# The branch gates' projection in two column halves, low-rank values in four strips, and layer norm's variance in two parts, in a hybrid decoder trunk on one core

## The chip, the cores and the metric

The kernel runs on one core of one Trainium2 chip. The metric is device time of one execution in microseconds (us). The profile is one execution taken by the hardware profiler. Engines are called PE (TensorE, with PEld for its weight loads), DVE (VectorE), ACT (ScalarE), POOL (GpSimd) and SP (SyncE); SP and POOL issue DMAs here. TensorE's clock has two levels, 1.2 and 2.4 GHz; the profile gives the granted clock as a share of the higher one.

## The reference

Two layers (DEPTH = 2) of a decoder trunk, over 256 prompt tokens and 8 sample tokens that share every weight, T = 264 tokens in all, model width D = 2048. Cut to what the change touches:

```python
h = x @ w_in                                   # all mixers and gates at once
gates = sigmoid(gl)                            # gl: 48 columns of h, 3 branches x 16 heads
v = v + (v_first - v) * sigmoid(v0 + (v @ rw_v1) @ rw_v2)   # layer 1 only; rw_v1 is 1024 x 32
merged = sigmoid(g_A) * (o_A @ w_up_a) + sigmoid(g_B) * (o_B @ w_up_b)
x = layer_norm(ALPHA * x + merged @ w_out, g, b)            # over the 2048 channels

def layer_norm(x, g, b):
    mu = x.mean(-1)
    var = square(x - mu).mean(-1)
    return (x - mu) * rsqrt(var + LN_EPS) * g + b
```

## The kernel before

All activations stand transposed: channels on the 128 partitions, the 264 tokens along the free axis. `XT` holds x as KT = 16 tiles of 128 x 264, `H` the projected tiles, everything in float32. A tile of output channels is 16 matmuls (one per tile of the contraction) with 128 x 128 weights and 264 moving columns, accumulated in one of two banks of `PB` (bank 6 or 7 by the tile's parity). A layer has 126 such tiles in a fixed order (`TILES`): `lo`, 8 `v`, 8 `k`, 8 `r`, 8 `z`, 12 `kv`, `gl`, 8 `q`, 8 `zb`, 16 `gb`, 16 `ga`, 16 `up`, 16 `out`. In the trace a float32 matmul has two records.

**The order of the work.** SP streams the weights of one tile after another, in two halves, into two slots of `WT`; a slot is loaded again when the tile that used it is done. PE executes one written list: `project(place)` (L502) issues weight matmuls until a count `UPTO[place]`, which `plan()` works out beforehand; between two such calls stand the small matmuls of the mixers, of the attention and of the norms. So projection matmuls lie as cover between the steps of chains that go from PE to ACT or DVE and back. Each of PE, ACT, DVE and POOL runs its list in order and waits on counting semaphores.

**Branch gates.** Tile `gl` has 48 wanted columns and is computed with 128 x 48 weights. Its 16 matmuls fall in the third of four rounds of the recurrent mixer: two in the step after the second chunk's state, then four groups of three, then two, each group between the small matmuls of L667, L673 and L679 to L686 of one chunk and those of the next. ACT copies the tile to `H`, and after the mixer it takes tanh of it into `SG` (L1050); DVE makes sigmoid of that (L1357). Behind the tanh, ACT stages rows for the attention's compressed blocks (L929, eight copies) and then copies four transposed tiles of values (`VT`), for the first of which PE waits before it transposes the second.

**Low-rank values.** In layer 1, PE multiplies eight `v` tiles by the 128 x 32 tiles of `V1` (L539), all into the same 32 partitions, then sums squares of keys per head (L544, eight matmuls that are already spread over the four strips of 32 columns). ACT copies the 32 rows out; later they are the moving operand of `V2W`, with a contraction of 32 (L579). Behind L544 come DVE's maximum, ACT's square root (L980), DVE's reciprocal (L1222) and PE's L550, with ten projection matmuls as cover.

**Layer norm.** In the `out` stage DVE adds each tile of PSUM to the scaled `XT` (L1603) and keeps a running sum of tiles `LSUM` (L1611). After the last tile come, one behind the other:

```python
mm(PB[:, 0, 0:T], cm(ONES), LSUM[:, :], start=True, stop=False)      # L915
mm(PB[:, 0, 0:T], cm(ONES), XT[:, KT - 1, :], start=False, stop=True)  # L916: sum over channels
# DVE, four instructions of four tiles: XT -= PB[0] / D          (L1616)
# ACT, four instructions of four tiles: LSQ = XT squared         (L1161)
# PE, sixteen matmuls of ONES with the tiles of LSQ into bank 1  (L920)
# DVE: bank 1 / D + LN_EPS (L1618); ACT: sqrt (L1163); DVE: reciprocal (L1620)
# DVE: XT *= 1/std in parts of 1, 3, 4, 4, 4 tiles (L1624)
# ACT: gain and bias, tile by tile                               (L1167)
```

In layer 0, matmul k of the next layer's first tile (`lo`) waits for the gain and bias of tile k. After layer 1, POOL stores y in the same five parts, each when ACT is done with it.

Of the kernel before, what the change touches and what calls it, by code (L numbers as in the profile page):

```python
# [9 lines left out]
ALU = mybir.AluOpType  # L10
# [39 lines left out]
N_DER = 65  # L50
# [46 lines left out]
def plan():  # L97

    upto = {}
    for L in range(DEPTH):  # L100
# [12 lines left out]
        upto[L, "up"] = first + FIRST["out"] * KT  # L113
        upto[L, "out"] = first + N_TILES * KT
# [47 lines left out]
def hybrid_trunk(nc, ins, outs):  # L162
# [4 lines left out]
    with ExitStack() as ctx:  # L167
# [129 lines left out]
        LSQ, LST, LSUM = take(P, KT, T), take(P, T), take(P, T)  # L297

# [14 lines left out]
        def steps(phase, rounds, **engines):  # L313
            for e, names in engines.items():
# [4 lines left out]
        steps("par", 1, v="om half ka")  # L319
# [6 lines left out]
        steps("mix", DEPTH, a="tanh gates pick", t="v0 v1 v2 v3 gates pick", v="gate")  # L326
# [45 lines left out]
        def _(sp):  # L372
# [4 lines left out]
            for n in range(DEPTH * N_TILES):  # L377
# [4 lines left out]
                for half in range(2):  # L382
# [4 lines left out]
                    if n == 0 and half == 1:  # L387
                        load_x(3)

        @block.gpsimd  # L390
        def _(po):
# [83 lines left out]
            for i, j in parts:  # L475
                on(po, "ln_a", DEPTH - 1, f"aff{j - 1}")
                dma(y_t[:, i:j, :], XT[:, i:j, :], st_y)
            po.wait_ge(st_y, 80)
# [7 lines left out]
        def _(pe):  # L486
# [44 lines left out]
            for L in range(DEPTH):  # L531
# [1210 lines left out]
```

## Time and profile before

| | us |
|---|---|
| median of 3 runs (lowest to highest) | 2359.83 (2357.12 to 2361.86) |
| the profiled execution, its own time | 2359.26 |
| its span, first to last instruction | 2357.6 |
| PE busy | 2292.0 (97%) |
| weight loads (PEld) busy | 1853.9 |
| DVE busy | 635.9 (27%) |
| ACT busy | 358.2 (15%) |
| POOL busy | 131.8 (6%) |
| mean granted clock of TensorE | 0.990 |

Busy time is the union of an engine's records. The chain that ended last is followed back from the last instruction to what released each step; its shares tell which engine the end of the program hangs on. The stretches with PE idle are few and short, and the ends of the two layers are the longest of them.

### The profile page before, as it was taken

How to read it: one execution, taken by the hardware profiler on the slowest of the kernel's cores; microseconds unless marked ns; L12 is line 12 of the kernel's file. 1: busy time of each engine (PE TensorE's matmuls, PEld its weight loads, DVE VectorE, ACT ScalarE, POOL GpSimd, SP SyncE). 2: the span in 40 equal slices, each digit the busy share in tenths (PEclk: the TensorE clock that was granted, in tenths of full speed). 3: DMA queues.
4: the chain of work that ended last, by engine and by line, in shares of the span. 5: the costliest groups of instructions: out<-in, count | busy, mean ns of one | idle time of the engine just before them, and what ended most of it. 6: DMA issues, size and time to landing. Idle time of an engine off the chain costs nothing.

```text
span 2357.6 us, 39271 instructions
## 1 busy us (share of the span) xinstructions
PE 2292.0 (97%) x17604; PEld 1853.9 (79%) x17604; DVE 635.9 (27%) x1156; ACT 358.2 (15%) x939; POOL 131.8 (6%) x233
## 2 busy tenths in 40 slices
PE   8999999999999999999899999999999999999995
PEld 7887878778786788888788778777788767888884
DVE  0133322227316310111201424223363253001112
ACT  0111111120104311000201211111211052100002
POOL 0000000011011210000000000000101103000000
PEclk9999999999999999999999999999999999999997
DMA  6533333346333454444344332333554325444441
GB/s 217 182 124 99 121 126 109 127 147 241 131 119 103 149 174 145 153 144 147 102 148 143 107 110 97 122 107 112 202 205 144 106 91 173 149 152 152 143 143 73
DMA packets 86792, 326.41 MB, mean 138 GB/s; under 512 B 11808, under 2 KB 11824, under 8 KB 84448
## 3 DMA queue, kind: packets, MB, share of 16 engines
q1 hardware_dynamic: 73152, 266.44, 33.9%
q0 software_dynamic: 13472, 57.46, 6.9%
q8 instruction: 139, 2.28, 0.4%
q14 instruction: 29, 0.24, 0.0%
HBM read 313.42 MB, written 18.82 MB: 141 GB/s over the span
## 4 chain that ended last, share of the span: by engine, by line
PE 95%; DVE 2%; ACT 2%; DMA 1%; issue 0%; POOL 0%; DVEq 0%; ACTq 0%; SPq 0%; POOLq 0%
PE PB L521 76%; PE PB L762 3%; PE PB L593 1%; PE PB L491 1%; PE PB L636 1%; PE PB L650 1%; PE PB L809 1%; PE PB L920 1%; PE PB L854 1%; ACT ARENA L929 1%; DMA WT<-in_w_all 1%; PE PB L673 1%; PE PB L679 1%; PE PB L667 0%; PE PB L806 0%
## 5 line engine op out<-in xcount | busy, mean ns | idle before, releaser
L521 PE MATMUL PB<-XT,WT 128*128 128x264 f32 (+1 forms) x6016 | 1422.6, 392 | 13.5 <-DMA WT<-in_w_all 7.0
L521 PEld LDWEIGHTS PB<-XT,WT 128*128 128x128 f32 (+1 forms) x6016 | 1119.9, 190 | 237.1 <-issue 36.1
L521 PE MATMUL PB<-H,WT 128*128 128x264 f32 x2048 | 456.5, 386 | 3.1 <-DVE H L1595 3.1
L521 PEld LDWEIGHTS PB<-H,WT 128*128 128x128 f32 x2048 | 389.0, 190 | 70.3 <-issue 3.8
L929 ACT ACTIVATE ARENA<-PB 128x512 f32<-128x512 f32 (+5 forms) x197 | 88.6, 475 | 357.0 <-PE PB L625 115.1
L1592 DVE SCALAR_TENSOR_TENSOR H<-H,PB 128x264 f32<-128x264 f32 x32 | 13.7, 430 | 305.2 <-PE PB L521 305.2
L1195 DVE COPY SHO<-PB 128x9 f32<-128x9 f32 x66 | 11.0, 167 | 266.2 <-ACT H L951 214.7
L393 POOL DMA_DIRECT2D out<-in_c_win x16 | 8.2, 512 | 1279.0 <-DVE ARENA L1350 1279.0
L1161 ACT ACTIVATE ARENA<-XT 128x1056 f32<-128x1056 f32 x8 | 8.7, 1084 | 458.4 <-DVE XT L1616 458.0
L951 ACT ACTIVATE H<-PB,PD 128x264 f32<-128x264 f32 x58 | 27.9, 480 | 287.9 <-PE PB L521 287.9
L1603 DVE SCALAR_TENSOR_TENSOR XT<-PB,XT 128x264 f32<-128x264 f32 x32 | 13.9, 433 | 207.1 <-PE PB L521 207.1
L966 ACT ACTIVATE H<-PB 128x264 f32<-128x264 f32 x64 | 25.0, 391 | 293.7 <-PE PB L521 293.5
L762 PE MATMUL PB<-ARENA 128*128 128x288 f32 x256 | 62.9, 407 | 2.2 <-ACT ARENA L929 2.2
L762 PEld LDWEIGHTS PB<-ARENA 128*128 128x128 f32 x256 | 48.5, 190 | 16.2 <-ACT ARENA L929 3.0
L1112 ACT ACTIVATE ARENA<-ARENA 128x128 f32<-128x128 f32 (+1 forms) x128 | 56.4, 445 | 23.1 <-DVE ARENA L1510 23.1
L393 POOL DMA_DIRECT2D ARENA<-in_c_sel x64 | 40.1, 627 | 294.5 <-issue 294.5
L1331 DVE TENSOR_TENSOR ARENA<-ARENA,PB 128x1024 f32<-128x1024 f32 x32 | 39.1, 1222 | 58.7 <-PE PB L653 58.7
L957 ACT ACTIVATE H<-PB 128x264 f32<-128x264 f32 x56 | 21.8, 390 | 214.2 <-PE PB L521 214.2
L1350 DVE SCALAR_TENSOR_TENSOR ARENA<-PB,ARENA 128x64 f32<-128x64 f32 x64 | 15.2, 279 | 144.0 <-PE PB L679 143.8
L1322 DVE TENSOR_TENSOR ARENA<-ARENA,CM 128x512 f32<-128x512 f32 x32 | 22.2, 692 | 88.2 <-PE PB L625 63.3
L636 PEld LDWEIGHTS PB<-ARENA 64*64 64x64 f32 x1024 | 32.6, 134 | 11.0 <-issue 11.0
L650 PEld LDWEIGHTS PB<-ARENA 64*64 64x64 f32 x1024 | 32.3, 134 | 11.0 <-issue 8.3
(277 smaller groups left out, 1685.9 us busy)
## 6 DMA issues: line engine op xcount, KB each, us to landing
WT<-in_w_all SPq DMA_DIRECT2D x504, 512.0 KB, 4.7
out<-in_c_win POOLq DMA_DIRECT2D x16, 512.0 KB, 5.4
ARENA<-in_c_cmp POOLq DMA_DIRECT2D x64, 128.0 KB, 4.2
ARENA<-in_c_sel POOLq DMA_DIRECT2D x64, 128.0 KB, 3.3
ARENA<-in_c_win POOLq DMA_DIRECT2D x32, 256.0 KB, 3.7
ARENA<-in_states POOLq DMA_DIRECT2D x4, 1024.0 KB, 9.2
out<-ARENA POOLq DMA_DIRECT2D x4, 1024.0 KB, 4.5
ARENA<-in_w1d POOLq DMA_DIRECT2D x4, 1024.0 KB, 5.1
```

What stands on the lines that cost most here:

```text
L393: po.dma_start(out, in_).then_inc(s, 16)
L491: return tr(out, in_, ident[0:in_.shape[0], 0:in_.shape[0]])
L521: ins = mm(PB[0:m, bank, 0:T], WT[:, s, k, 0:m], x, start=start, stop=stop)
L593: ins = mm(PB[ra, 2 + 2 * w + i, c * P:c * P + P], src[ra, w, c * C:c * C + C], AR[ra, w * NCH + c].rearrange("p x n -> p (x n)"), start=T ...
L636: ins = mm(PB[ra, 0, q * C:q * C + C], LM[oa, q, :], XX[oa, q, :], start=True, stop=True)
L650: mm(PB[other(ra), 4, cols], XX[ra, 2 * NCH + q, :], YY[ra, q, :], start=True, stop=True)
L762: ins = mm(PB[:, 3 * (s // 8) + gp, 0:CMP_N], W1D[:, s, :], x, start=s % 8 == 0, stop=s % 8 == 7)
L929: return act(out, in_, ACT.Copy)
L951: act(a_tile(L, kind, t), psum, ACT.Copy, scale=PD[:, L, OM + t:OM + t + 1]).then_inc(scaled, 1)
L966: act(H[:, t if kind == "ga" else GB_AT[t], :], psum, ACT.Tanh, scale=0.5).then_inc(tile_out[s], 1)
L1112: ins = act(x, x, ACT.Exp, bias=NM[u % 3][:, t, i:i + 1], accum_out=RSM[u % 3][:, t, i:i + 1])
L1331: v(f"z{j}", tt(XX[:, :, :], XX[:, :, :], z, ALU.add))
```

## The change

Four things are done.

- **Branch gates.** Tile `gl` is computed with 64 weight columns (48 wanted, 16 zeros), even k into output rows 0 to 63, odd k into rows 64 to 127. ACT copies all 128 rows out. Before the tanh, ACT copies the lower 48 rows of the second half into `SG` and DVE adds the first half to it.
- **Low-rank values.** The eight matmuls of L539 go to four strips of 32 output rows, so that `VV1` has 128 rows with four partial sums, and `V2W` is stored four times below itself: the contraction of L579 has 128 rows.
- **Layer norm.** After `out` tile 12, PE sums the first 12 tiles (HEAD = 12) over the channels ("head"). DVE subtracts the mean of these 1536 channels from them into `LSQ`, ACT squares that, and after eight matmuls of tile 14 PE adds the twelve up in four strips of 32 columns, three each ("hvar"). ACT scales this by 1/32 into `LVA`, and after four matmuls of tile 15 PE sums it with ONES over all partitions, which starts bank 1 ("fold"). After the last tile: the sum as before; DVE centres tiles 12 to 15 first, in two instructions; ACT squares them in two; DVE makes the shift of the mean and its square times 1536 ("d", "e"); PE adds four matmuls of squares and one of the shift with the identity to bank 1; DVE meanwhile centres tiles 0 to 11 in three instructions. ACT's square root reads PSUM with LN_EPS as its bias and 1/D as its scale, and L1618 is gone. Gain and bias of tiles 12 to 15 move from ACT to DVE, behind the last of L1624.
- **Stores.** y goes out from SP's queue instead of POOL's, in parts of 3, 3, 3, 3 and 4 tiles.

```diff
@@ plan
+        out = first + FIRST["out"] * KT
+        upto[L, "head"], upto[L, "hvar"], upto[L, "fold"] = out + (HEAD + 1) * KT, out + (HEAD + 2) * KT + 8, out + (HEAD + 3) * KT + 4
@@ sync
+            for i, j in stores:
+                if j <= SPLIT:
+                    on(sp, "ln_a", DEPTH - 1, f"aff{j - 1}")
+                else:
+                    on(sp, "ln_v", DEPTH - 1, "affv")
+                sp.dma_start(y_t[:, i:j, :], XT[:, i:j, :]).then_inc(st_y, 16)
@@ tensor, project
+                    if kind == "gl":
+                        rows, start, stop = slice(k % 2 * C, k % 2 * C + C), k < 2, k >= KT - 2
+                    ins = mm(PB[rows, bank, 0:T], WT[:, s, k, 0:rows.stop - rows.start], x, start=start, stop=stop)
@@ tensor
-                        ins = mm(PB[0:32, 1, 0:T], V1[:, k, :], H[:, V0 + k, :], start=k == 0, stop=k == 7)
+                        ins = mm(PB[32 * (k % 4):32 * (k % 4) + 32, 1, 0:T], V1[:, k, :], H[:, V0 + k, :], start=k < 4, stop=k >= 4)
...
+                project(L, "head")
+                on(pe, "ln_v", L, f"sum{HEAD - 1}")
+                mark("ln_t", L, mm(PB[:, 2, 0:T], cm(ONES), LSUM[:, :], start=True, stop=True), "head")
+                project(L, "hvar")
+                for k in range(HEAD):
+                    on(pe, "ln_a", L, f"hq{k // 4}")
+                    rows = slice(32 * (k % 4), 32 * (k % 4) + 32)
+                    ins = mm(PB[rows, 3, 0:T], cm(ONES)[:, 0:32], LSQ[:, k, :], start=k < 4, stop=k >= HEAD - 4)
+                mark("ln_t", L, ins, "hvar")
+                project(L, "fold")
+                on(pe, "ln_a", L, "hv")
+                mm(PB[:, 1, 0:T], cm(ONES), LVA[:, :], start=True, stop=False)
...
-                for k in range(KT):
-                    if k % 4 == 0:
-                        on(pe, "ln_a", L, f"sq{k // 4}")
-                    ins = mm(PB[:, 1, 0:T], cm(ONES), LSQ[:, k, :], start=k == 0, stop=k == KT - 1)
-                mark("ln_t", L, ins, "var")
+                for k in range(HEAD, KT):
+                    on(pe, "ln_a", L, f"sq{(k - HEAD) // 2}")
+                    mm(PB[:, 1, 0:T], cm(ONES), LSQ[:, k, :], start=False, stop=False)
+                on(pe, "ln_v", L, "e")
+                mark("ln_t", L, mm(PB[:, 1, 0:T], ident, LDQ[:, :], start=False, stop=True), "var")
@@ scalar
-                mark("mix_a", L, act(SG[:, :], H[0:48, GL, :], ACT.Tanh, scale=0.5), "tanh")
+                mark("mix_a", L, copy(SG[:, :], H[C:C + 48, GL, :]), "half")
+                on(sc, "mix_v", L, "gl")
+                mark("mix_a", L, act(SG[:, :], SG[:, :], ACT.Tanh, scale=0.5), "tanh")
...
+                mark("ln_a", L, act(LST[:, :], PB[:, 1, 0:T], ACT.Sqrt, bias=PD[:, L, EPS:EPS + 1], scale=1.0 / D), "sqrt")
@@ vector
+                own("mix_a", "half")
+                mark("mix_v", L, tt(SG[:, :], SG[:, :], H[0:48, GL, :], ALU.add), "gl")
...
+                for q in range(2):
+                    centred(HEAD + 2 * q, 2, f"ycb{q}")
+                mark("ln_v", L, stt(LDA[:, :], PB[:, 0, 0:T], -1.0 / D, LMA[:, :], ALU.mult, ALU.add), "d")
+                own("ln_v", "d")
+                mark("ln_v", L, stt(LDQ[:, :], LDA[:, :], HEAD * P, LDA[:, :], ALU.mult, ALU.mult), "e")
+                for q in range(3):
+                    centred(4 * q, 4, f"yca{q}")
...
+                own("ln_v", "yn4")
+                for t in range(SPLIT, KT):
+                    ins = ts(XT[:, t, :], XT[:, t, :], PT[:, L, LNG + t:LNG + t + 1], PT[:, L, LNB + t:LNB + t + 1], ALU.mult, ALU.add)
+                mark("ln_v", L, ins, "affv")
```

## Rows read from the trace of the kernel before

**Rows 1.** The page: the chain that ended last, shares of the span by engine

```profile
PE 95%; DVE 2%; ACT 2%; DMA 1%; issue 0%; POOL 0%; DVEq 0%; ACTq 0%; SPq 0%; POOLq 0%
```

**Rows 2.** Chain of waits, end of layer 0: start us, us, what

```profile
1139.90 9.80 PE PB L521 x44
...
1150.08 0.43 DVE ARENA L1611
...
1150.64 0.68 PE PB L915 x2
...
1154.24 7.40 PE PB L920 x32
...
1162.59 1.81 DVE ARENA L1620
...
1165.65 10.51 PE PB L521 x38
```

**Rows 3.** Timeline, end of layer 0: start us, us, engine, line, operation, count, idle before

```profile
1151.81 4.75 DVE L1616 SCALAR_TENSOR_TENSOR XT<-PB,XT 128x1056 f32<-128x1056 f32 x4 [1.31 <-PE PB L916]
...
1157.70 1.28 ACT L1163 ACT_TABLE_LOAD   x1
...
1164.42 4.83 DVE L1624 TENSOR_TENSOR XT<-XT,ARENA 128x264 f32<-128x264 f32 x5
...
1174.92 0.48 ACT L951 ACTIVATE H<-PB,PD 128x264 f32<-128x264 f32 x1 [1.54 <-PE PB L521]
```

**Rows 4.** Timeline, end of layer 1

```profile
2319.84 0.43 DVE L1603 SCALAR_TENSOR_TENSOR XT<-PB,XT 128x264 f32<-128x264 f32 x1 [6.35 <-PE PB L521]
...
2324.36 10.12 PE L920 MATMUL PB<-ARENA,CM 128*128 128x264 f32 x32 [2.46 <-ACT ARENA L1161]
...
2335.43 1.80 DVE L1620 RECIPROCAL ARENA<-ARENA 128x264 f32<-128x264 f32 x1 [0.49 <-ACT ARENA L1163]
...
2338.64 7.59 ACT L1167 ACTIVATE XT<-XT,PT 128x264 f32<-128x264 f32 x15 [0.29 <-DVE XT L1624]
...
2346.63 0.53 POOL L393 DMA_DIRECT2D out<-XT  x1 [1.46 <-ACT XT L1167]
```

**Rows 5.** Windows: us; busy of PE, PEld, DVE, ACT, POOL; granted clock; DMA share; GB/s

```profile
1165.00:1170.00 5.00, 4.35 (x12) 3.13 (x13) 4.26 (x4) 4.71 (x10) 0.00 (x0) 0.66 0.00 0
...
2324.00:2326.00 2.00, 1.64 (x4) 1.33 (x5) 2.00 (x3) 1.84 (x3) 0.00 (x0) 0.50 0.00 0
2348.00:2349.00 1.00, 0.00 (x0) 0.00 (x0) 0.00 (x0) 0.00 (x0) 0.00 (x0) 0.50 1.00 418
```

**Rows 6.** Groups by line and form: busy us, mean ns

```profile
L1397 DVE SCALAR_TENSOR_TENSOR H<-PB,H 128x528 f32<-128x528 f32 x2 | 1.4, 708 | 2.5 <-PE PB L728 2.5
...
L1080 ACT ACTIVATE ARENA<-H 128x528 f32<-128x528 f32 x2 | 1.3, 644 | 0.9 <-DVE H L1397 0.9
```

**Rows 7.** Windows from a group's first start to the next group's (L736, L854)

```profile
598.29:599.32 1.03, 1.03 (x17) 0.41 (x17) 0.00 (x0) 1.03 (x1) 0.00 (x0) 1.00 0.00 0
734.61:735.09 0.48, 0.48 (x5) 0.34 (x6) 0.41 (x1) 0.48 (x3) 0.00 (x0) 1.00 0.00 0
```

**Rows 8.** Window: a `gl` group (L521's PE, PEld, clock, DMA); timeline: an uncovered L673

```profile
420.17:421.64 1.47, 1.47 (x6) 0.66 (x6) 1.00 0.94 228
...
512.64 0.45 PE L673 MATMUL PB<-ARENA 64*64 64x64 f32 x8 [0.38 <-ACT ARENA L929]
```

**Rows 9.** Layer 1: window over L539 and L544, then timeline, ACT and DVE

```profile
1295.80:1300.36 4.56, 4.56 (x33) 2.20 (x32) 0.96 (x4) 3.77 (x7) 0.00 (x0) 1.00 0.67 225
...
1296.80 1.28 ACT L974 ACT_TABLE_LOAD   x1
...
1301.73 1.80 DVE L1222 RECIPROCAL ARENA<-ARENA 128x264 f32<-128x264 f32 x1 [0.78 <-ACT ARENA L980]
```

**Rows 10.** Timeline behind the mixer of layer 0, ACT and PE

```profile
518.32 3.41 ACT L929 ACTIVATE ARENA<-H 64x128 f32<-64x128 f32 x8 [0.62 <-PE PB L491]
...
522.43 0.52 PE L491 MATMUL PB<-CM,H 128*128 128x128 f32 x3 [1.59 <-ACT VT L929]
```

More of the change, by code:

```diff
@@ L49 @@
 OM, W0H, A0H, V0H, KA1 = 0, 33, 41, 49, 57
-N_DER = 65
+N_DER = 66
+EPS = 65
+HEAD = 12
+SPLIT = 12
 IDENT, ONES, BLOCK = 0, 1, 2
@@ L297, in hybrid_trunk @@
         LSQ, LST, LSUM = take(P, KT, T), take(P, T), take(P, T)
+        LMA, LDA, LDQ, LVA = (take(P, T) for _ in range(4))
         d_const, d_par, d_toep, d_lora, d_w1, d_page = (sem(n) for n in (
@@ L325, in hybrid_trunk @@
                             + " ".join(f"lm{j + 1} z{j}" for j in range(1, LEVELS)) + f" z{LEVELS} st " + " ".join(f"d{c} s{c}" for c in ch)))
-        steps("mix", DEPTH, a="tanh gates pick", t="v0 v1 v2 v3 gates pick", v="gate")
+        steps("mix", DEPTH, a="half tanh gates pick", t="v0 v1 v2 v3 gates pick", v="gl gate")
         steps("mixv", DEPTH, a="v0 v1 v2 v3")
@@ L338, in hybrid_trunk @@
         steps("xa", DEPTH, a="scale")
-        steps("ln", DEPTH, t="mu var", v=" ".join(f"sum{i}" for i in range(1, KT - 1)) + " " + " ".join(f"yc{q}" for q in range(4)) + " eps rs "
-              + " ".join(f"yn{q}" for q in range(5)), a=" ".join(f"sq{q}" for q in range(4)) + " sqrt " + " ".join(f"aff{i}" for i in range(KT)))
+        steps("ln", DEPTH, t="head hvar mu var", v=" ".join(f"sum{i}" for i in range(1, HEAD)) + " hm" + "".join(f" hc{q}" for q in range(3)) + " "
+              + " ".join(f"sum{i}" for i in range(HEAD, KT - 1)) + " ycb0 ycb1 d e" + "".join(f" yca{q}" for q in range(3)) + " rs "
+              + " ".join(f"yn{q}" for q in range(5)) + " affv", a="hq0 hq1 hq2 hv sq0 sq1 sqrt " + " ".join(f"aff{i}" for i in range(SPLIT)))
         parts = [(0, 1), (1, 4), (4, 8), (8, 12), (12, 16)]
+        stores = [(0, 3), (3, 6), (6, 9), (9, 12), (12, 16)]
         def on(eng, key, it, name):
@@ L473, in _ @@
                         dma(SVS[odd][:, m, 2:4, :], c_win[L, b, :, 2:4, :], d_att[odd])
[L475 to L478, printed above, removed]
+            po.wait_ge(st_y, 16 * len(stores))
             po.wait_ge(st_shift, DEPTH * 16)
@@ L510, in project @@
                     if kind == "lo" and L:
-                        on(pe, "ln_a", L - 1, f"aff{k}")
-                    m, bank, start, stop = P, 6 + s, k == 0, k == KT - 1
+                        if k < SPLIT:
+                            on(pe, "ln_a", L - 1, f"aff{k}")
+                        else:
+                            on(pe, "ln_v", L - 1, "affv")
+                    rows, bank, start, stop = slice(0, P), 6 + s, k == 0, k == KT - 1
                     if kind == "up":
@@ L1667, in packed @@
     out["lora"] = c(np.concatenate([i["rw_w2"], i["rw_a2"]], 1))
-    out["v2w"] = c(i["rw_v2"][0])
+    out["v2w"] = c(np.tile(i["rw_v2"][0], (4, 1)))
     out["v1"] = c(i["rw_v1"][0].reshape(8, P, 32).transpose(1, 0, 2))
```

52 lines of the change are left out of this document (33 added, 19 removed).

## The prediction

> **What bounds the kernel now.** I read the page's chain first: 95% of the span hangs on PE [rows 1]. A microsecond is gained only where PE issues less, or where it stands idle waiting for a chain of other engines. Next the chain of waits at the end of layer 0, which shows the price of a projection matmul, 9.80/22 = 0.445 us (two records each), and the longest stretch without projection work: the last `out` matmul ends at 1149.70, L915 starts at 1150.64, and `lo` starts at 1165.65, 15.95 us later [rows 2]. In it PE works 1.15 + 7.40 us and otherwise waits. The timeline gives the steps beside the chain [rows 3], the end of layer 1 the same chain ahead of the stores [rows 4], the windows the granted clock [rows 5]. Then I looked for what the trace shows of matmuls side by side in strips of the array [rows 7], and at the places of the two small edits [rows 8 to 10].
>
> The sum is made against the profiled execution's own 2359.26 us (its span is 2357.6). That is 0.57 below the median of the runs shown. Their spread is 4.7 us, and 0.2%, about what a measurement of this kernel can tell from no change, is 4.7 us too.
>
> **Branch gates.** A group of three narrow matmuls takes 1.47 us, as three full ones would (3 x 0.445 and the joints), so 48 columns save nothing now [rows 8]. Do halves run side by side? Two matmuls of 128 x 64 weights and 256 columns took 0.48 us from start to the next group, where one alone needs 256/264 x 0.445 = 0.43; eight in four strips with 264 columns took 1.03, two rounds of 0.445 and 0.14 for the joints [rows 7]. So I count rounds. The sixteen matmuls fall in groups of 2, 3, 3, 3, 3, 2; alternating halves make each one round shorter: 6 x 0.445 = 2.67. For joints I take off 0.17 and use 2.5 a layer, **-5.0** in all (ends: -5.3, and 0 if halves don't overlap). The groups are cover for copies on ACT. Where nothing covers such a copy, PE stands idle 0.38 ahead of L673 [rows 8]; a group of about 1.0 still covers that.
>
> The trace shows the joint of a switch to strips and back at about 0.07 each. The Trainium skill ("TensorEngine Tiling (Array Packing)", Key Properties) says that changing the tiling mode, unlike changing the tile, drains TensorE. The trace agrees that a joint costs something. If a drain costs more at the new joints than at those of rows 7, the time is the second rival's, 2352.0; by the sum it is 2347.0.
>
> The price of this edit is one ACT copy, one DVE addition and two hand-overs ahead of the tanh: 0.43 (a neighbour's 3.41/8 [rows 10]), 0.43 (L1611 [rows 2]) and 0.04, so 0.9 us. ACT stands idle for 0.62 behind the tanh, until PE has transposed the state's vectors, so 0.28 shows. Behind it are queued eight copies, 3.41, then the copy of the first value tile for which PE already waits 1.59 [rows 10]. **+0.6** for two layers (0 to 1.8, if the cover of 0.62 were gone). DVE's copies behind its own part come up to 0.9 later, and what follows them waits for states by DMA. POOL's and SP's queues are not touched here.
>
> **Low-rank values (layer 1).** L539 and L544 together take 4.56 us; as two groups of eight in strips they take 2 x 1.03: -2.5 [rows 7, 9]. What is late next: L544 needs the last square, ready at 1296.8, early enough. But ACT's queue (table load from 1296.80, tanh, two copies, table load, square root) no longer fits. With 1.28 for a load and some 0.42 for each of the others the root ends near 1301.05, the reciprocal (1.80) near 1302.9, while PE, ten matmuls behind 1297.9, stands there at 1302.6: +0.3. Net **-2.2** (-2.5 to -1.5; 0 without overlap). The eight matmuls of L579 go from 32 to 128 rows with the same columns: 0, and for the range 0.19 each way for each, the weight load that such a joint may show or hide.
>
> **Layer norm, inside the `out` stage.** New on PE, per layer. "Head" stands at a tile's boundary and needs DVE's addition and running sum of the tile just finished; that is the wait ahead of L915, 1150.64 - 1149.70 = 0.94 idle, and 0.445 for the matmul [rows 2]. "Hvar" is twelve in four strips, 1.03 + 0.445 = 1.48 [rows 7]; its squares are ready in time, since DVE (0.43 and 3 x 1.2) and ACT need some 6 us and 24 matmuls (10.7) lie between. "Fold" is 0.445. With joints 3.4, **+6.8** for two layers. The ends are 3.3 and, if strips ran one after another, 12 x 0.445 + 1.9 = 7.2 a layer. Weights are no issue: SP's loads hang on finished tiles as before.
>
> **The end of layer 0.** Count from the last `out` matmul, t = 0. The sum is done at 2.1 as before. DVE then has two centrings of 528 columns, 0.708 each [rows 6], "d" and "e", 0.43 each, and three centrings of 1056; four of those take 4.75, so a step is 1.17 [rows 3]. With issue overlaps: 2.1 + 0.65 + 0.65 + 0.46 + 0.36 + 3.6 = 7.8. Meanwhile ACT squares at 2.9 and 3.5, 0.64 each [rows 6]; PE starts at 3.6, five matmuls with the closing latency of L920 (7.40 - 7.12) end at 6.1; ACT's table load (1.28 [rows 3]) is done at 5.5; the root ends at 6.5. DVE is later: the reciprocal starts at **7.8**, and DVE takes PE's place as what the end hangs on. Before it was 1162.59 - 1149.70 = 12.9 [rows 2]. The rest, to `lo`'s first matmul, is 3.06 in both. **-5.05**.
>
> The granted clock: `lo` runs from 1165.65 to 1174.90, 9.25 instead of 7.12. The clock is at 1.2 GHz from shortly after its start (0.66 over 1165 to 1170, so 3.4 us low, 1.7 lost [rows 5]); the rest is the wait for the second tile's gain. PE had stood idle 4.0 us before it. After the change it stands idle 10.9 - 6.1 = 4.8, and the clock may be down already when `lo` starts. I take +0.5. The ends are -1.7 (no low stretch) and +1.0 (a loss like that of L920 in layer 1, 10.12 - 7.40 = 2.7 [rows 2, 4]).
>
> **The end of layer 1.** Before, the clock fell in the gap ahead of L920, and sixteen matmuls took 10.12 instead of 7.40 [rows 2, 4, 5]; the reciprocal started at 2335.43 - 2319.80 = 15.6. After: 7.8 at the high clock; at the low one five matmuls cost 2.2 more, 1.0 of which shows beyond DVE, 8.8. The first gap is shorter now (1.5 us instead of 2.5), so I take 8.1: **-7.5**. Behind the reciprocal's start ACT takes up its second tile at 3.2 and ends tile 11 at 3.2 + 11 x 0.51 = 8.9; DVE ends its last scaling at 1.84 + 4.83 = 6.7 [rows 3, 4] and tiles 12 to 15, at 0.43 each at most, by 8.4. Before, ACT ended at 10.8 [rows 4]. The last data moved until 2349.0, 13.6 after the reciprocal's start [rows 4, 5]. Now two stores of together 0.95 MB leave almost at once at 8.9. At 418 GB/s [rows 5] that is 2.3, with a start like SP's weight loads, 1.0 to 2.0 behind the issue: 12.3 to 13.3. **-0.6** (-1.3 to +0.5).
>
> By the Trainium skill ("DMA: Bandwidth & Descriptors", SWDGE vs HWDGE) first bytes come in about 0.6 us from SP against about 1 us from POOL, an estimate of 0.4 us less. No run here yet shows a store from SP.
>
> **The sum:** -5.0 + 0.6 - 2.2 + 6.8 - 5.05 + 0.5 - 7.5 - 0.6 = -12.45, so 2359.26 - 12.45 = 2346.8; with a part of the distance to the median, **2347.0**.
>
> **Rivals.**
> - *The clock eats part of it* (10%). Both ends run their five matmuls at 1.2 GHz and `lo` has the long low stretch: +1.0, +0.7 and +0.5, so 2349.2. For it: the drop in rows 5 in a gap of 2.5. Against it: layer 0 had the same gap and stayed high.
> - *Joints cost more than I take* (8%). If each of the six `gl` groups and every other new joint loses about 0.25, a matmul's tail, that is 12 groups of `gl` and some 8 other places, 20 x 0.25 = 5.0: 2352.0. Against: 0.14 for a whole group [rows 7].
> - *Less at the ends than the sum has* (8%): the clock stays up in `lo`, stores overlap better and strips lose nothing: -2.2, -0.7, -0.5, so 2343.6.
> - *Slower* (3%): matmuls of new strips don't run side by side because they accumulate in one bank. It decides at the first group of `gl`: -5.0 and -2.2 fall away, "hvar" costs 3.8 more twice: 2347.0 + 7.2 + 7.7 = 2361.9, slower than before by 2.6, and 2364.1 with the clock's 2.2. Both groups of rows 7 speak against it, and both accumulate in strips of one bank.
> - *The change doesn't do what it says* (2%): the ends stay, because the root still comes last behind something (a second table load, 1.28): then some 2 us less gain, 2349.
>
> **How the numbers follow.** The forecast has 69%. The bounds of its terms, not all at once, give 2342 to 2352; the rivals of the same sign lie inside or near. Range 2341.5 to 2353, about 8 in 10 with the spread of a median. Faster by over 0.2% needs less than 2355: 0.90, within 0.2% 0.07, slower 0.03.
>
> **What would show it.** Steps: `gl`'s groups at 1.0 us; L539's successor and L544 in 2.1 with a wait of some 0.3 before L550; PE idle 0.9 before "head" in each layer; DVE without a gap from the sum to the reciprocal, which starts 7.8 behind the last `out` matmul. Wrong: ACT's root ending later than DVE's last centring, a first `gl` group still at 1.47, `lo` above 11 us, or the last store landing more than 14 behind the reciprocal.

## The result, and the profile of the changed kernel

The changed kernel takes **2346.82 us** (median of five runs), the one before 2360.61 (five runs, 2357.12 to 2362.08): a ratio of 0.9942 with a 95% interval of 0.993 to 0.9953, so 13.8 us faster by the medians. Four of the five runs of the changed kernel lie between 2345.11 and 2347.16 (their own median is 2346.78); the fifth took 4759.01 us, was slow for a reason that nothing on record shows, and is not in the ratio. The profiled execution took 2347.16 us (span 2345.5), where the one of before took 2359.26 (span 2357.6): 12.1 us less in both, against a sum of 12.45.

The page's chain answers to [rows 1]. PE holds 94% of it. POOL and its queue, in the chain before, are gone from it, since the stores now go through SP's queue:

```profile
PE 94%; DVE 2%; ACT 2%; DMA 1%; issue 0%; ACTq 0%; SPq 0%; DVEq 0%
```

In the new file L521 is L540, L539 and L544 are L559 and L564, L550 is L570, L915/L916/L920 are L948/L949/L952, L1611/L1616/L1620/L1624 are L1659/L1671/L1682/L1686, L1163/L1167 are L1205/L1210, L929 is L962, L491 is L505.

The end of layer 0, timeline (start us, us, engine, line, operation, count, idle before); it answers to [rows 2, 3]:

```profile
1153.16 0.68 PE L948 MATMUL PB<-ARENA,CM 128*128 128x264 f32 x2 [0.96 <-DVE ARENA L1659]
...
1154.33 1.32 DVE L1671 SCALAR_TENSOR_TENSOR XT<-PB,XT 128x528 f32<-128x528 f32 x2 [1.31 <-PE PB L949]
1155.07 1.26 ACT L1203 ACTIVATE ARENA<-XT 128x528 f32<-128x528 f32 x2 [13.73 <-DVE XT L1671]
...
1155.77 3.51 PE L952 MATMUL PB<-ARENA,CM 128*128 128x264 f32 x8 [1.48 <-ACT ARENA L1203]
...
1159.75 0.48 ACT L1205 ACTIVATE ARENA<-PB,PD 128x264 f32<-128x264 f32 x1 [2.13 <-PE PB L954]
1160.27 1.80 DVE L1682 RECIPROCAL ARENA<-ARENA 128x264 f32<-128x264 f32 x1 [0.31 <-ACT ARENA L1205]
...
1163.32 13.05 PE L540 MATMUL PB<-XT,WT 128*128 128x264 f32 x45 [3.61 <-ACT XT L1210]
```

And the end of layer 1, which answers to [rows 4]:

```profile
2319.54 1.32 DVE L1671 SCALAR_TENSOR_TENSOR XT<-PB,XT 128x528 f32<-128x528 f32 x2 [1.31 <-PE PB L949]
...
2320.78 0.42 DVE L1676 SCALAR_TENSOR_TENSOR ARENA<-PB,ARENA 128x264 f32<-128x264 f32 x1
...
2320.98 2.05 PE L952 MATMUL PB<-ARENA,CM 128*128 128x264 f32 x8 [1.48 <-ACT ARENA L1203]
2321.23 0.43 DVE L1678 SCALAR_TENSOR_TENSOR ARENA<-ARENA 128x264 f32<-128x264 f32 x1
...
2321.58 3.58 DVE L1671 SCALAR_TENSOR_TENSOR XT<-PB,XT 128x1056 f32<-128x1056 f32 x3
...
2323.51 0.48 ACT L1205 ACTIVATE ARENA<-PB,PD 128x264 f32<-128x264 f32 x1 [0.67 <-PE PB L954]
2325.08 1.79 DVE L1682 RECIPROCAL ARENA<-ARENA 128x264 f32<-128x264 f32 x1
...
2328.27 5.59 ACT L1210 ACTIVATE XT<-XT,PT 128x264 f32<-128x264 f32 x11 [0.29 <-DVE XT L1686]
2329.40 5.29 SPq L404 DMA_DIRECT2D out<-XT  x5
```

The same code runs twice, and the two places differ in one row: the eight records of L952 take 3.51 in layer 0 and 2.05 in layer 1. In layer 1 no DVE row carries an idle time from L1671's first to the reciprocal at 2325.08, and the root ended at 2323.99, 1.1 earlier: DVE sets the end. In layer 0 the root came last, and the reciprocal waited for it (0.31 idle, ACT named).

The windows (columns as in [rows 5]) show why the eight records differ; 1155 to 1160 against 2320 to 2324, then the start of the next layer, then the stores:

```profile
1155.00:1160.00 5.00, 3.95 (x10) 2.85 (x10) 4.92 (x7) 2.79 (x4) 0.00 (x0) 0.66 0.33 134
...
1165.00:1170.00 5.00, 5.00 (x15) 3.92 (x15) 3.33 (x6) 4.06 (x9) 0.00 (x0) 0.60 0.00 0
...
2320.00:2324.00 4.00, 2.49 (x10) 1.82 (x10) 3.97 (x7) 3.02 (x4) 0.00 (x0) 1.00 0.00 0
2336.00:2337.00 1.00, 0.00 (x0) 0.00 (x0) 0.00 (x0) 0.00 (x0) 0.00 (x0) 0.50 1.01 410
```

Where the 12.1 us come from, by stretches between the same events in both profiled executions (us):

| stretch | before | after | difference |
|---|---|---|---|
| layer 0: start to the last mixer matmul | 517.06 | 514.70 | -2.36 |
| to the first gate selection (tanh chain) | 13.41 | 14.03 | +0.62 |
| to the `out` stage | 504.37 | 504.92 | +0.55 |
| `out` stage | 114.85 | 118.55 | +3.70 |
| last `out` matmul to the reciprocal | 12.90 | 8.07 | -4.83 |
| first gain to the end of `lo`'s first tile | 9.99 | 10.97 | +0.98 |
| layer 1: low-rank values | 9.21 | 7.20 | -2.01 |
| mixer | 381.69 | 378.75 | -2.94 |
| tanh chain, and what follows up to `out` | 518.26 | 518.44 | +0.18 |
| `out` stage | 114.84 | 118.57 | +3.73 |
| last `out` matmul to the reciprocal | 15.63 | 7.67 | -7.96 |
| reciprocal to the end of the span | 22.17 | 20.42 | -1.75 |

The two stretches left out (2.30 ahead of the first gain, 120.9 ahead of the values) are the same within 0.02.

### The profile page after: what moved, and what is told of

It is laid out like the page before. It is cut to its first block, busy times and chain, and to the rows that moved or that the text cites. A ratio compares the mean times of both kernels' runs of the same rounds, so it can differ in the third digit from the quotient of the medians.

```text
span 2345.5 us, 39317 instructions
## 1 busy us (share of the span) xinstructions
PE 2282.0 (97%) x17616; PEld 1847.0 (79%) x17616; DVE 648.1 (28%) x1179; ACT 355.9 (15%) x937; POOL 128.7 (5%) x228
## 4 chain that ended last, share of the span: by engine, by line
PE 94%; DVE 2%; ACT 2%; DMA 1%; issue 0%; ACTq 0%; SPq 0%; DVEq 0%
PE PB L540 76%; PE PB L782 3%; PE PB L505 1%; PE PB L613 1%; PE PB L670 1%; PE PB L656 1%; PE PB L829 1%; PE PB L874 1%; ACT ARENA L962 1%; DMA WT<-in_w_all 1%; PE PB L693 1%; PE PB L699 1%; PE PB L687 0%; PE PB L826 0%; PE PB L596 0%
## 5 line engine op out<-in xcount | busy, mean ns | idle before, releaser
L540 PE MATMUL PB<-XT,WT 128*128 128x264 f32 (+1 forms) x6016 | 1418.6, 392 | 13.7 <-DMA WT<-in_w_all 6.9
L540 PEld LDWEIGHTS PB<-XT,WT 128*128 128x128 f32 (+1 forms) x6016 | 1119.2, 190 | 233.9 <-issue 34.8
L540 PE MATMUL PB<-H,WT 128*128 128x264 f32 x2048 | 457.7, 386 | 3.1 <-DVE H L1641 3.1
L540 PEld LDWEIGHTS PB<-H,WT 128*128 128x128 f32 x2048 | 388.8, 190 | 71.0 <-issue 4.7
L962 ACT ACTIVATE ARENA<-PB 128x512 f32<-128x512 f32 (+5 forms) x197 | 88.5, 475 | 353.2 <-PE PB L645 115.2
L1638 DVE SCALAR_TENSOR_TENSOR H<-H,PB 128x264 f32<-128x264 f32 x32 | 13.7, 429 | 305.2 <-PE PB L540 305.2
L1649 DVE SCALAR_TENSOR_TENSOR XT<-PB,XT 128x264 f32<-128x264 f32 x32 | 13.8, 433 | 204.8 <-PE PB L540 204.8
L1197 ACT ACTIVATE ARENA<-ARENA 128x1056 f32<-128x1056 f32 x6 | 6.5, 1084 | 415.5 <-DVE ARENA L1665 415.2
```

The source lines that it names most:

```text
L540: ins = mm(PB[rows, bank, 0:T], WT[:, s, k, 0:rows.stop - rows.start], x, start=start, stop=stop)
L962: return act(out, in_, ACT.Copy)
```

## The experiments

Those of one group share their runs of the kernel before; each is set against the change (2346.82, ratio 0.9942) and read by its stretches too. The medians of the kernel before lie between 2359.78 and 2362.13 in the groups, so differences of 1 or 2 us between medians are not settled by them, and the intervals of all ratios here but one (the twelve squares at full width) overlap with the change's. Such readings rest on the stretches of one profiled execution each.

**Layer norm undone.** The kernel before with only the two narrow edits (column halves and quarters).

```diff
 kernel before, plus
+ rows, start, stop = slice(k % 2 * C, k % 2 * C + C), k < 2, k >= KT - 2
+ mm(PB[32*(k%4):32*(k%4)+32, 1, 0:T], V1[:, k, :], ..., start=k < 4, stop=k >= 4)
 ...   # the longer chain ahead of the tanh, VV1 and V2W with 128 rows
```

> The kernel before with the two narrow edits alone (gates in halves, values in strips); layer norm and the stores as before. Theory, the sum of parts: 2359.3 - 5.1 + 0.6 to 1.0 - 2.0, so 2352.9; the change of the norm is then worth about 6 us of the 12 to 13. Rival, the norm's two parts give nothing once their matmuls in the out stage are paid (3.7 a layer): 2347. Other rival, the narrow edits give nothing: 2359.

Measured: 2351.97 us (seven runs, 2347.45 to 2354.15; ratio 0.9965, 0.9952 to 0.9977; before 2359.78). The two narrow edits bring 7.8 us by the medians, and the layer norm with the stores the other 5.2. Its `out` stage is 114.84 in both layers and the reciprocal stands 12.90 and 14.59 behind, so all of these lengths belong to the layer norm's edit. Its tail from the reciprocal on is 22.11: the stores' gain belongs to it as well. The last step of layer 1 is 1.0 shorter than before with the same instructions; it is one of those that the clock decides (below).

**Gates in one tile.**

```diff
-rows, start, stop = slice(k % 2 * C, k % 2 * C + C), k < 2, k >= KT - 2
+rows = slice(0, 48)
-mark("mix_a", L, copy(SG[:, :], H[C:C + 48, GL, :]), "half")
-on(sc, "mix_v", L, "gl")
-mark("mix_a", L, act(SG[:, :], SG[:, :], ACT.Tanh, scale=0.5), "tanh")
+mark("mix_a", L, act(SG[:, :], H[0:48, GL, :], ACT.Tanh, scale=0.5), "tanh")
 ...   # DVE's addition goes, ACT copies 48 rows out
```

> The changed kernel with the branch gates put back into one 48-column tile (and no addition ahead of the tanh). Theory, the step as predicted: each of the twelve groups of the gates' matmuls grows by 0.43 (1.03 to 1.47), 5.1 in all, and the stretch behind the mixer gets back what the longer chain ahead of the tanh costs, 0.3 a layer: about 4.5 slower than the changed kernel, 2351.5. Rival, the longer chain ahead of the tanh costs much more than 0.3 a layer (layer 0 lost 0.86 between the last small matmuls of the mixer and the transposed gates): then only 3.4 slower, 2350.4. The stretch itself tells them apart: 13.6 us as before the change, by both; with the granted clock at 1.00 in it by the theory that the clock and not the chain took the rest.

Measured: 2350.84 us (five runs, 2349.72 to 2351.62; 0.9961, 0.9947 to 0.9975): 4.0 more than the change; every run of it lies above every one of the change's four (2347.16 at most), though the intervals overlap. The mixer of layer 1 takes 381.32 against 378.75, 2.57 for six groups. The tanh chain is 13.41 and 13.40, and 13.71 in both layers of most runs with the halves: the hand-overs cost 0.30. In the change's profiled run it was 14.03 and 13.88. The extra 0.3 and 0.2 are the clock (0.50 over 514 to 516, 0.66 over 1680 to 1685), not the chain: the other runs with halves have 13.7 or 14.0 by where the clock stands.

**Low-rank values in one strip.**

```diff
-mm(PB[32*(k%4):32*(k%4)+32, 1, 0:T], V1[:, k, :], H[:, V0+k, :], start=k < 4, stop=k >= 4)
+mm(PB[0:32, 1, 0:T], V1[:, k, :], H[:, V0+k, :], start=k == 0, stop=k == 7)
 ...   # VV1 and V2W with 32 rows again
```

> The changed kernel with the eight low-rank matmuls put back into one strip of 32 rows and a contraction of 32 behind them. Theory, as predicted: the two groups of eight take 4.56 instead of 1.92, the wait of 0.56 ahead of the broadcast of key norms is gone, net 2.0 slower than the changed kernel, 2348.8. Rival, the sixteen-fold partial sums (128 rows of contraction) cost something in the four rounds of the mixer in layer 1: then less than 2.0, with the pairs of matmuls around them more than 0.01 apart from the changed kernel's.

Measured: 2349.05 us (four runs, 2348.4 to 2350.22; 0.9953, 0.9936 to 0.9969), 2.2 more than the change, again with every run above the change's; the stretch of the values takes 9.21 against 7.20. The timeline of the change there:

```profile
1294.45 1.10 PE L559 MATMUL PB<-H,V 128*32 128x264 f32 x16
...
1295.37 1.07 PE L564 MATMUL PB<-ARENA,CM 128*32 128x264 f32 x16
...
1299.79 1.80 DVE L1266 RECIPROCAL ARENA<-ARENA 128x264 f32<-128x264 f32 x1 [2.85 <-ACT ARENA L1013]
1301.65 1.16 PE L570 MATMUL PB<-ARENA,CM 32*128 32x264 f32 x12 [0.56 <-DVE ARENA L1266]
```

Eight matmuls of 32 columns take 0.92 from start to start (1294.45 to 1295.37), where one strip took 3.5. The wait that follows them, 0.56 ahead of the broadcast of the key norms, is the new limit: ACT's two table loads, copies and root and DVE's reciprocal end last there, so a still faster pair of groups would only lengthen it.

The expectation's rival, that a contraction of 128 rows costs something in the mixer's rounds, is settled the other way round. The group of twelve small matmuls that holds L579 (L599 now), one in each of four rounds, is shorter with 128 rows. Windows from its first start to the next projection matmul in the second round, the kernel before (32 rows) and the change (128 rows):

```profile
1410.45:1413.02 2.57, 2.57 (x14) 1.19 (x13) 0.00 (x0) 0.00 (x0) 1.74 (x4) 1.00 1.16 464
...
1407.09:1409.57 2.48, 2.48 (x13) 1.39 (x13) 0.00 (x0) 0.00 (x0) 1.74 (x4) 1.00 1.22 494
```

It is 2.57 again in this run, and 2.48 in the run with the gates in one tile; the four groups make 0.33. Why is not shown.

**Stores on POOL's queue again.**

```diff
-sp.dma_start(y_t[:, i:j, :], XT[:, i:j, :]).then_inc(st_y, 16)
+dma(y_t[:, i:j, :], XT[:, i:j, :], st_y)    # on POOL, same waits
```

> The changed kernel with its five stores of y issued by GpSimd again, same parts, same waits. From the reciprocal's start in layer 1 to the end of the span it was 22.2 before and is 20.4 now. Theory, the gain is partly the queue (0.4 us from a tile's end to the issue on GpSimd, 0.53 an issue): 21.0 to 21.5, the kernel 0.6 to 1.1 slower than the changed one. Rival, the gain is that four tiles went from ScalarE to VectorE, and the queue gives nothing: 20.4, no difference.

Measured: 2346.25 us (four runs, 2344.68 to 2348.02; 0.9941, 0.9924 to 0.9957), which by medians can't be told from the change; but the tail is clock-free and comes out the same each time. From the reciprocal to the end of the span it is 21.30, where the change has 20.42 and the kernel before 22.17. So 0.88 of the tail's gain is the queue. The other 0.87 belongs to the four tiles that no longer stand behind ACT and to the new parts of the stores together; no run separates them. The last issues on POOL, and the landing times (KB each, us from issue to landing):

```profile
2332.68 1.09 POOL L403 DMA_DIRECT2D out<-XT  x2 [0.95 <-ACT XT L1209]
...
out<-XT POOLq DMA_DIRECT2D x1, 528.0 KB, 3.5
```

against the change's:

```profile
out<-XT SPq DMA_DIRECT2D x4, 396.0 KB, 2.4
...
out<-XT SPq DMA_DIRECT2D x1, 528.0 KB, 3.3
```

With POOL, ACT's last tile ended at 2332.28; the issue of the last two stores began 0.40 later and took 0.54 for each, and the data flowed until 2336.25, 3.97 behind ACT. With SP, ACT's last tile ended at 2333.86 and the data at 2337.0, 3.1 behind it.

**Head's matmul under cover.** It goes three projection matmuls behind the tile's boundary.

```diff
-upto[L, "head"] = out + (HEAD + 1) * KT
+upto[L, "head"] = out + (HEAD + 1) * KT + 3
```

> The changed kernel with the matmul of the first twelve tiles' sum moved three projection matmuls into the next tile, so that they cover VectorE's addition and running sum. Theory: the idle of 0.86 ahead of it in each layer goes, the out stage takes 117.7 instead of 118.55 in each, 1.7 in all. Rival: the wait comes back further on (the squares of the twelve are then 1.3 late for their matmuls): 118.5.

Measured: 2344.65 us (four runs, 2342.11 to 2346.57; 0.993, 0.9907 to 0.9953; before 2361.64). The `out` stage takes 117.41 against 118.55, in both layers: 1.14 each. The idle time that the change shows ahead of it is gone. The change's rows there:

```profile
1125.64 1.50 PE L540 MATMUL PB<-H,WT 128*128 128x264 f32 x6
1128.01 0.71 PE L933 MATMUL PB<-ARENA,CM 128*128 128x264 f32 x2 [0.87 <-DVE ARENA L1659]
1128.56 1.72 PE L540 MATMUL PB<-H,WT 128*128 128x264 f32 x7
```

Counted from start to start, the stop cost more than its 0.87 idle. Six records from 1125.64 on, 0.2225 apart, would have let the next one start at 1126.98; it started at 1128.01, 1.03 later. "Head" then took 0.55 to the next start instead of 0.445, 0.10 more. Together that is the 1.14. A record lasts 0.39 and the next one starts 0.22 behind its start, so the idle time between records is less than what is lost.

Not all of it was kept. In this profiled run the five matmuls between the squares and the root ran at the low clock in both layers, and the reciprocal stands 8.29 behind the last `out` matmul in both, where the change has 8.07 and 7.67; `lo` takes 11.1:

```profile
1157.42 1.80 DVE L1682 RECIPROCAL ARENA<-ARENA 128x264 f32<-128x264 f32 x1 [0.54 <-ACT ARENA L1205]
```

**Reciprocal ahead of the last centring.** DVE's queue reordered, nothing else.

```diff
-sum.. ycb0 ycb1 d e yca0 yca1 yca2 rs yn0 yn1 yn2 yn3 yn4
+sum.. ycb0 ycb1 d e yca0 yca1 rs yn0 yn1 yn2 yca2 yn3 yn4
```

> The changed kernel with VectorE's last centring (tiles 8 to 11) moved behind the reciprocal and three of the scalings. Theory, VectorE's queue is what the end of a layer hangs on when the clock is high: in layer 1 the reciprocal starts 6.6 behind the last out matmul instead of 7.67, and the span ends some 0.5 earlier; in layer 0, if the five matmuls run at 1.2 GHz there, the root itself is late and the reciprocal stays at 8.05. Rival, the root comes last in both: no difference anywhere.

Measured: 2345.28 us (four runs, 2344.46 to 2346.98; 0.9939, 0.9916 to 0.9961). The timeline of its profiled run, PE and DVE in layer 0, then PE in layer 1:

```profile
1154.13 2.05 PE L951 MATMUL PB<-ARENA,CM 128*128 128x264 f32 x8 [1.48 <-ACT ARENA L1202]
...
1157.17 1.80 DVE L1681 RECIPROCAL ARENA<-ARENA 128x264 f32<-128x264 f32 x1
...
2317.76 3.46 PE L951 MATMUL PB<-ARENA,CM 128*128 128x264 f32 x8 [1.48 <-ACT ARENA L1202]
```

Where the clock was high (layer 0) the reciprocal stands 6.60 behind the last `out` matmul, 1.07 earlier than 7.67: DVE's queue was the bound there. Where it was low (layer 1) it stands at 8.02, as in the change's layer 0: there DVE's order is worth nothing, and PE's five matmuls are the bound. That shows both halves of the mechanism, in the other layers than expected: where the clock falls was not foreseen. `lo` takes 9.80 here behind the same 3.61 us of idle PE, since the low spell was over earlier (0.66 over 1160 to 1165, then 1.00).

**The twelve squares at full width.** Instead of the four strips and "fold".

```diff
-ins = mm(PB[rows, 3, 0:T], cm(ONES)[:, 0:32], LSQ[:, k, :], start=k < 4, stop=k >= HEAD - 4)
+ins = mm(PB[:, 1, 0:T], cm(ONES), LSQ[:, k, :], start=k == 0, stop=False)
-mm(PB[:, 1, 0:T], cm(ONES), LVA[:, :], start=True, stop=False)
```

> The changed kernel with the twelve squares added up by full-width matmuls straight into the variance's bank; the four strips, ScalarE's scaling and the folding matmul are gone. Theory, strips work side by side: 12 x 0.445 = 5.34 instead of 1.47 + 0.45, the out stage takes 122.0 instead of 118.55 in each layer, 6.8 slower in all, 2353.7. Rival, the joints around the strips and the folding eat half of what they save: 120, 3 slower.

Measured: 2352.28 us (eight runs, 2350.43 to 2355.18; 0.9968, 0.9955 to 0.9981), 5.5 more than the change. The `out` stage takes 121.76, 3.2 a layer more. The chain of waits has the twelve here (two records each):

```profile
1137.33 5.34 PE PB L937 x24
```

and in the change the twelve in strips, then "fold":

```profile
1139.40 1.48 PE PB L938 x24
...
1146.42 0.45 PE PB L943 x2
```

5.34 is 12 x 0.445, and 1.48 is three rounds of 0.445 and 0.145 for the joints, for the same products. The strips work side by side, also where they accumulate in one bank. But the stage grew by 3.21 only, so strips and "fold" cost 5.34 - 3.21 = 2.13 together, 0.2 more than the 1.48 + 0.445 of their records: the joints cost that much beside them.

**Unread matmuls in PE's idle gaps.** Three between the sum over the channels and the squares (the gap of 1.5), and in layer 0 eight behind the last one (the gap that ends at `lo`). Nothing reads their result.

```diff
+for k in range(3):
+    mm(PB[:, 5, 0:T], ident, CM[:, 0:T], start=True, stop=True)
 ...
+if L + 1 < DEPTH:
+    for k in range(8):
+        mm(PB[:, 5, 0:T], ident, CM[:, 0:T], start=True, stop=True)
```

> The changed kernel with matmuls that nobody reads: three between the sum and the squares in both layers, eight behind the variance in layer 0, into an unused bank. Theory, the clock falls because TensorE stands idle in the gaps at the end of a layer: with the gaps filled the five matmuls of layer 0 run at 2.4 GHz (reciprocal at 7.67 instead of 8.07) and the first tile of layer 1 too (from the first gain to its last matmul 8.6 instead of 10.9): 2.3 to 2.7 faster. Rival, it is the tile's waits for gain and bias that make it long: 10.9 stays. Other rival, the filler delays what follows by a matmul at each place: up to 1.3 slower.

Measured: **2341.65 us** (four runs, 2340.92 to 2343.21; 0.9923, 0.9901 to 0.9946), below every run of the change (by the ratios 4.5 us faster than the change, with overlapping intervals). Windows of its profiled run:

```profile
1155.00:1160.00 5.00, 4.53 (x21) 3.53 (x19) 4.97 (x6) 0.94 (x3) 0.00 (x0) 1.00 0.00 0
...
1165.00:1170.00 5.00, 5.00 (x23) 3.98 (x23) 1.09 (x5) 1.84 (x4) 0.00 (x0) 1.00 0.04 9
```

The clock stays at 2.4 GHz where it fell to 0.66 and 0.60 in the change. The reciprocal stands 7.67 behind the last `out` matmul in both layers, and `lo`'s first tile takes 9.09 instead of 10.97. By stretches that is 2.3 less. The other 2.9 of the medians lie in stretches without an edit (gates to `out`: 502.99 and 503.06 here, 504.92 and 504.56 in the change), where the low clock covers less time in this run than in the change's; whether the unread matmuls brought that is not shown.

**Unread matmuls in the second gap alone**, against the kernel with both:

```diff
-for k in range(3):
+for k in range(0):
```

> The changed kernel with the eight filler matmuls behind the variance of layer 0 alone; the gap of 1.48 ahead of the squares stays open in both layers. Theory, idleness in the longer gap is what makes the first tile of layer 1 slow: from the first gain to its end 9.1 instead of 10.97, and the five matmuls ahead of it stay open to a fall (2.05 or 3.5 for the first four): 1.9 faster than the changed kernel, 2344.9. Rival, both gaps are needed to keep the clock up: 10.9 stays.

Measured: 2344.7 us (six runs, 2343.37 to 2345.97; 0.9931, 0.992 to 0.9943; before 2362.13). `lo`'s first tile takes 9.09, as with both, while the reciprocal stands at 8.07 and 8.14. So the second gap decides the start of `lo`: in the three profiled runs with it filled the tile takes 9.1 to 9.3, in the eight with the new layer norm and the gap open 9.8 to 11.2. For the first gap the evidence is weaker. With it open, the five matmuls between squares and root ran at the low clock at 9 of 18 ends of a layer, and at the high one at the others (both ends with the gates in one tile, with the stores on POOL, and with the twelve at full width); with it filled, at none of four.

**All three: head covered, reciprocal first, unread matmuls.**

```diff
-upto[L, "head"] = out + (HEAD + 1) * KT
+upto[L, "head"] = out + (HEAD + 1) * KT + 3
-yca0 yca1 yca2 rs yn0 yn1 yn2 yn3 yn4
+yca0 yca1 rs yn0 yn1 yn2 yca2 yn3 yn4
+for k in range(3): ...   # and range(8) in layer 0, as above
```

> The changed kernel with three things together: the twelve tiles' sum three matmuls later, the last centring behind the reciprocal, and the filler matmuls in both gaps. Theory, by the stretches of the single runs: out stage 117.4 instead of 118.55 twice (-2.3), reciprocal at 6.6 instead of 8.07 in layer 0 (-1.5) and 7.67 in layer 1 (-1.1, of which 0.5 reaches the last store), the first tile of layer 1 9.1 instead of 10.97 (-1.9): 6.2 less than the changed kernel's 2346.8, so 2340.6. Rival, VectorE's later scalings hold up the first tile and the last store: then no better than the fillers alone, 2341.7.

Measured: **2341.53 us** (five runs, 2337.02 to 2341.88; 0.9918, 0.9905 to 0.9931). It is faster than the kernel before and the change: 5.3 less than the change by medians, 5.7 by the ratios. The stretches show all three gains (`out` 117.41 and 117.42, reciprocal at 6.61 and 6.60, `lo` 9.25), but against the unread matmuls alone the median is only 0.1 better and the ratios' intervals overlap. What the two reorderings add to them is not shown by the times. 2340.6 had been expected.

**The two reorderings without unread matmuls.**

```diff
-for k in range(3): ...   # against the kernel with all three
-for k in range(8): ...
```

> As the run with all three, without the filler matmuls. Theory, the gaps then decide by the phase of the clock which of the two ends loses what the reordering gives: out stage -2.3, between -0.5 and -2 at the ends: 2343.3, with a wider spread of single runs than with the fillers. Rival, the clock is of no account: 2340.6 as with them.

Measured: 2346.33 us (six runs, 2341.17 to 2347.9; 0.9934, 0.9921 to 0.9948). `out` is 117.41 in both layers, but the reciprocal stands at 8.29 and 8.29: in this run the five matmuls ran at 1.2 GHz at both ends, so its reordering brought nothing there (8.29 stood also in the run with "head" covered and DVE's old order), and the mean clock was 0.987. 2343.3 had been expected, 3.0 less. A spread of 6.7 us, and a median that can't be told from the change's. Where the clock is lost, the gain of the reciprocal is lost with it. Both profiled runs with "head" covered and the gap open lost the clock at both ends, the other seven at 5 of 14; that covering "head" causes the loss is not shown.

## Why the prediction was right

The forecast was 2347.0 and the median is 2346.82; the likeliest case came, by its mechanisms, with several terms off by 0.2 to 1.2 that nearly cancel. That the two numbers lie within 0.2 us is luck: the gates (with 0.33 of L579's), the end of layer 1 and the tail gained 1.9 more than their terms, the tanh chain, the values, the `out` stages, the end of layer 0 and `lo` lost 2.0 more, an unedited stretch lost 0.25 by the clock, and medians of the kernel before differ by over 2 us between the groups. One of the prediction's own signs of being wrong came: in layer 0 ACT's root ended later than DVE's last centring.

- **Branch gates, -5.0:** right. The first group of `gl` takes 1.03 where it took 1.47 [rows 8], the joint as read from rows 7:

```profile
419.53:420.56 1.03, 1.03 (x10) 0.47 (x6) 0.00 (x0) 0.28 (x1) 0.00 (x0) 1.00 0.86 187
```

 Six groups make 2.57 in layer 1. In layer 0 the stretch is 2.2 shorter than in the run with the gates in one tile (516.89 to 514.70), and up to 3.2 in other runs (513.74). Only part of that spread is the clock: the run with the unread matmuls had no low spell there and took 514.68.
- **The tanh chain, +0.6:** right in mechanism and size, 0.30 a layer against 0.28. The eight copies that started at 518.32, 0.62 behind PE [rows 10], now start 0.21 behind:

```profile
515.49 0.43 DVE L1401 TENSOR_TENSOR ARENA<-ARENA,H 48x264 f32<-48x264 f32 x1 [1.14 <-ACT ARENA L962]
...
515.95 0.42 ACT L1085 ACTIVATE ARENA<-ARENA 48x264 f32<-48x264 f32 x1 [0.49 <-DVE ARENA L1401]
...
516.59 3.40 ACT L962 ACTIVATE ARENA<-H 64x128 f32<-64x128 f32 x8 [0.21 <-PE PB L505]
...
520.69 0.52 PE L505 MATMUL PB<-CM,H 128*128 128x128 f32 x3 [1.28 <-ACT VT L962]
```

 The profiled run paid 1.1 for both layers instead; 0.5 of that is the clock.
- **Low-rank values, -2.2:** -2.01. Both groups took 1.92 to the next projection matmul, a saving of 2.6 (predicted 2.5), and the wait ahead of the broadcast is 0.56, where 0.3 was expected: the table loads and roots on ACT came as listed, and ended 0.25 later relative to PE. The matmuls of L579 with 128 rows were taken at 0, with 0.19 each way for each; they gain 0.33 in all, 0.04 each. The kernel before and the run with the gates in one tile, both without a low spell in the mixer of layer 1, differ by 0.37 there (381.69 and 381.32).
- **Layer norm in the `out` stage, +6.8:** +7.4, under-sized by 0.3 a layer. "Hvar" is the predicted 1.48 and "fold" 0.445. The step that failed is "head": 0.94 + 0.445 = 1.39 was counted, and covering it shows 1.14 + 0.445 = 1.59. The idle time between the records is not all that a stop at a boundary costs, from start to start it is 1.03, and 0.10 behind it. The other 0.1 are joints: 0.2 by the full-width run, where 0.085 was counted.
- **The end of layer 0, -5.05:** -4.83. DVE was taken as the bound, 7.8, and is where the clock is high: 7.67. In the change's run it was not the bound here; the five matmuls ran at the low clock, the root came last, and the reciprocal stood at 8.07. The prediction priced that case for layer 1 and as a rival (8.8, "1.0 of which shows beyond DVE"); 0.4 show here, and 0.6 at most (8.29).
- **`lo`'s clock, +0.5:** +0.98, at the upper end of its bounds. The mechanism is as put: PE stands idle 3.61 ahead of the tile, and the clock is down over most of the tile (0.60 over 1165 to 1170). The unread matmuls show that this gap is the cause.
- **The end of layer 1, -7.5:** -7.96. The clock stayed high here, and 8.1 allowed for a part of its loss. Some of the gain is the clock of the kernel before: 15.63 holds its low spell, and the same instructions took 14.59 in the run with the layer norm undone.
- **Behind the reciprocal, -0.6:** -1.75, the term furthest off. ACT's last tile ended 8.8 behind the reciprocal's start, as predicted (8.9; its own sum, 3.2 + 11 x 0.51, gives 8.8), but the data was through at 11.9, not 12.3 to 13.3, and 0.6 was taken where the middle of that is 0.8. A start of 1.0 to 2.0 behind the issue was taken from SP's weight loads. By the window ahead of the full ones (share 0.52), the flow of the last stores took some 2.5 and so began about 0.6 behind ACT's end:

```profile
2334.00:2335.00 1.00, 0.00 (x0) 0.00 (x0) 0.00 (x0) 0.00 (x0) 0.00 (x0) 0.50 0.52 203
```

 The Trainium skill ("DMA: Bandwidth & Descriptors", Specifications) gives a first byte of about 0.6 us on SP's path and about 1 us on POOL's, by estimate 0.4 us between them. Here no data moved in the first 0.80 us behind SP's first issue of y and in the first 1.06 behind POOL's, and in both it flowed within the next 0.1: 0.3 between them. The tail as a whole differs by 0.88, in which POOL's issue time of 0.54 is contained.

Against the rivals: "joints cost more" falls with the group of 1.03 and the strips' 1.48, and with 0.2 a layer beside them. The Trainium skill ("TensorEngine Tiling (Array Packing)", Key Properties) says that changing the tiling mode drains TensorE; at the `gl` groups nothing shows above the 0.07 a joint of rows 7, and at the strips of "hvar" and at "fold" 0.2 a layer does. "Slower" falls with the full-width experiment: there the stage is 3.2 a layer longer. "The clock eats part of it" is half true: it did in layer 0, at the five matmuls (0.4) and in `lo` (1.0), and not in layer 1. "The change doesn't do what it says" falls with the reciprocal at 8.07 and 7.67, where it stood at 12.90 and 15.63. Of "less at the ends" only the stores came.

## What to carry to other kernels

Count matmuls that leave columns or rows of the array empty in rounds of side-by-side strips, and price the joint from a group the trace already has. Work taken from behind a reduction's last input pays even if it costs more in total (here +7.4 of PE time against -12.8 at the two ends), but look next at which queue then comes last, and at PE's idle gaps: a gap of a few microseconds can also cost clock behind it. Unread matmuls in two such gaps were worth 2.3 us by the stretches (5.2 by medians, but nothing shows that the rest came from them), as much as covering "head" in two layers (2.3 by the stretches, 2.2 by medians).

## What was not expected of the hardware

At the ends of the layers the granted clock falls in one run and stays up in the next. The same five matmuls behind the same gap of 1.48 ran at the low clock in layer 0 and at the high one in layer 1 of the change, and the other way round with the reciprocal moved. The Trainium skill ("TensorE: Matmul & The Clock Gate", Part 1) says that the number of matmuls at the low clock at a kernel's start varies between runs of one kernel; in the middle of a kernel it is so here too: the mean granted clock of one kernel lay between 0.988 and 0.993 in its seven runs (layer norm undone). It also falls where PE has no idle time by the records, as in this window of the change:

```profile
705.00:710.00 5.00, 5.00 (x19) 2.86 (x20) 3.24 (x13) 0.59 (x2) 3.77 (x7) 0.50 0.60 188
```

But that place is not a random one. It stands behind 64 matmuls of only 15 columns, in the attention over the compressed blocks, and a second one comes behind an idle time of 1.92 further on:

```profile
701.64 4.18 PE L814 MATMUL PB<-KCT,H 64*128 64x15 f32 x64
...
724.00 0.48 PE L826 MATMUL PB<-H 64*128 64x256 f32 x1 [1.92 <-DVE ARENA L1553]
```

Over the 13 profiled runs and both layers, the clock fell within 2.1 us of the last of the 64 in 22 of 26 cases, and within 1.4 us of the end of that idle time in 18 of 26 (in none of four with both end gaps filled). So the spells between the gates and `out` come at the same two places of the program, and what differs is whether they come and how long they last.

The stretch from gates to `out`, which no experiment edited, took between 502.97 and 505.64 us in the profiled runs: up to 504.9 where only one of the two places cost clock and briefly, 504.9 to 505.6 where both did at their longest. That the narrow matmuls themselves start the spells is suggested by their place and not shown: no run here was made for it. With unread matmuls at the two gaps the mean clock rose from 0.989 to 0.994, and the largest time fell to 2343.21; whether the later spells were fewer because of them, or by chance of four runs, was not settled either.
